# Narrower waits on the tensor engine, an interleaved first down product, and a second queue for x

## The reference

```python
h = rmsnorm(x, norm_mix_w);  proj = h @ w_in                # 24 groups of 512 columns here
go, S = gated_delta(conv(q,k,v), g, beta, S0)               # 8 heads, matrix state S
mh, C, n, m = mlstm(q, k, v, i, f, C0, n0, m0)              # 8 heads, state C and row n
mixed = sigmoid(gate_a) * (go @ w_branch_a) + sigmoid(gate_b) * (mh @ w_branch_b)
x = x + mixed @ w_out
f = rmsnorm(x, norm_ffn_w)
u, new_ffn_conv = causal_dwconv(f @ w_up, state_ffn_conv, ffn_conv_w)
x = x + (silu(u_gate) * u_val) @ w_down
y = rmsnorm(x, norm_final_w)                                # and all states are outputs
```

## Time and profile before

| | us |
|---|---|
| median of 3 runs | 1937.2 |
| the three runs | 1937.20, 1937.06, 1938.79 |
| the profiled execution's own time | 1938.22 |
| its span in the trace | 1936.3 |
| PE busy | 1898.7 (98%) |
| DVE busy | 1198.0 (62%) |
| ACT busy | 931.5 (48%) |
| mean granted clock of PE | 0.996 |

### The profile page before, as it was taken

How to read it: one execution, slowest core, us unless ns; L and a number is a source line. 1 busy time by engine, 2 the same in 40 slices (tenths; PEclk the granted TensorE clock), 3 DMA queues, 4 the chain that set the end, 5 groups by cost and what they waited for, 6 DMA issues and landing times.

```text
span 1936.3 us, 39112 instructions
## 1 busy us (share of the span) xinstructions
PE 1898.7 (98%) x14356; PEld 1855.5 (96%) x14356; DVE 1198.0 (62%) x2534; ACT 931.5 (48%) x1859; POOL 155.5 (8%) x324
## 2 busy tenths in 40 slices
PE   9999999999999999999999999999999999999996
PEld 8899999999999999999999999999999999999996
DVE  5766666666655666656655676754566664466742
ACT  5555455545534444445544544443454443354553
POOL 4000010001000110100022000000000000000021
PEclk9999999999999999999999999999999999999998
DMA  8555455555556666745755666656566656556552
GB/s 224 148 134 151 131 143 152 151 140 137 143 145 171 189 160 175 193 145 165 216 156 159 166 165 164 162 156 170 159 176 159 168 158 170 164 147 174 159 153 70
DMA packets 572607, 308.19 MB, mean 159 GB/s; under 512 B 10531, under 2 KB 567739, under 8 KB 572491
## 3 DMA queue, kind: packets, MB, share of 16 engines
q1 hardware_dynamic: 531943, 281.50, 53.6%
q10 hardware_dynamic: 40548, 25.13, 4.5%
HBM read 293.58 MB, written 13.02 MB: 158 GB/s over the span
## 4 chain that ended last, share of the span: by engine, by line
PE 83%; DVE 7%; issue 5%; ACT 4%; ACTq 1%; DVEq 1%; DMA 0%; SPq 0%; POOL 0%
PE products L1801 25%; PE products L1803 24%; PE products L1802 24%; PE mixer L1782 3%; DVE w_lo L585 2%; ACT w_hi L578 2%; PE mixer L1912 1%; PE mixer L1918 1%; DVE u_gate L1700 1%; DVE u_val L1700 1%; DVE u_padded L1690 1%; PE products L1986 0%; PE products L1960 0%; PE mixer L1864 0%; ACT conv_out L926 0%
## 5 line engine op out<-in xcount | busy, mean ns | idle before, releaser
L585 DVE TENSOR_TENSOR w_lo<-w_raw,w_hi 128x512 fp32r<-128x512 f32 x1037 | 717.6, 707 | 642.4 <-ACT w_hi L578 639.0
L578 ACT ACTIVATE w_hi<-w_raw 128x512 fp32r<-128x512 f32 x1037 | 628.5, 626 | 600.2 <-PE products L1803 572.5
L1801 PE MATMUL products<-h_hi,w_hi 128*128 128x288 f32 x1536 | 476.5, 310 | 0.0
L1802 PE MATMUL products<-h_lo,w_hi 128*128 128x288 f32 x1536 | 453.0, 295 | 0.0
L1803 PE MATMUL products<-h_hi,w_lo 128*128 128x288 f32 x1536 | 452.6, 295 | 0.0
L1801 PE MATMUL products<-f_hi,w_hi 128*128 128x288 f32 x1408 | 416.9, 296 | 0.0
L1802 PE MATMUL products<-f_lo,w_hi 128*128 128x288 f32 x1408 | 415.4, 295 | 0.0
L1803 PE MATMUL products<-f_hi,w_lo 128*128 128x288 f32 x1408 | 414.5, 294 | 0.0
L1801 PEld LDWEIGHTS products<-h_hi,w_hi 128*128 128x128 f32 x1536 | 289.2, 188 | 14.5 <-issue 10.4
L1802 PEld LDWEIGHTS products<-h_lo,w_hi 128*128 128x128 f32 x1536 | 289.1, 188 | 0.5
L1803 PEld LDWEIGHTS products<-h_hi,w_lo 128*128 128x128 f32 x1536 | 288.9, 188 | 0.0
(11 more groups left out here) (462 smaller groups left out, 2218.9 us busy)
## 6 DMA issues: line engine op xcount, KB each, us to landing
w_raw<-in_w_in SPq DMA_DIRECT2D x95, 1024.0 KB, 6.0
w_raw<-in_w_up SPq DMA_DIRECT2D x88, 1024.0 KB, 5.8
w_raw<-in_w_down SPq DMA_DIRECT2D x32, 1024.0 KB, 5.8
w_raw<-in_w_out SPq DMA_DIRECT2D x16, 1024.0 KB, 7.0
w_raw<-in_w_down SPq DMA_DIRECT2D x16, 768.0 KB, 4.8
w_raw<-in_w_branch_a SPq DMA_DIRECT2D x8, 1024.0 KB, 5.4
w_raw<-in_w_branch_b SPq DMA_DIRECT2D x8, 1024.0 KB, 5.5
S_sample<-in_state_gdn_S ACTq DMA_DIRECT2D x8, 512.0 KB, 7.4
```

What stands on the lines that cost most here:

```text
L578: nc.scalar.activation(ring_slot(whi, whi2, n, ring), raw[:, s % slots, 4 * j:4 * j + 4], ACT.Copy).then_inc(hi_ready, 1)
L585: nc.vector.tensor_tensor(ring_slot(wlo, wlo2, n, ring), raw[:, s % slots, 4 * j:4 * j + 4], ring_slot(whi, whi2, n, ring).bitcast(F32), A ...
L1801: mm(out, w_hi, x_hi, start=start, stop=False)
L1802: mm(out, w_hi, x_lo, start=False, stop=False)
```

## The change

Six edits, all in the order and in the waits of instructions; no arithmetic changes and only the order in which blocks are added into two banks differs.

1. **Start.** The eight small x loads of the samples are issued by ACT's queue, behind `norm_rows`; SP keeps the prompt's x and the weights.
2. **v_new.** ACT's copy of the first `v_new` becomes a lane of its own, ahead of `prepare`; the load of `S_sample` moves one slot later (`yield 1`).
3. **n.** PE turns n after the `ffn_w_rows` at the end of `w_out`, into banks 2 and 3; ACT copies and stores it there. PE's waits for the mLSTM's last steps move to the first uses (DVE's at the second product of a branch iteration, ACT's behind the branch stage), and `norm_sum` waits for `no_a.after("s")`.
4. **f_hi.** The five residual copies get a semaphore of their own (`ox_a`), and `turn_input` and the turn of `ffn_w_rows` wait for that one.
5. **down.** In the first group of each down product the first two column tiles are interleaved: (tile, j) runs (0,0) (0,1) (0,2) (1,0) (1,1) (1,2) (0,3) (1,3), then tiles 2 and 3 as before. ACT and DVE split the blocks in that order; DVE adds tile 0 up behind block 7 and tile 1 behind block 8; the reload of the first raw buffer waits for block 8 in place of 4 (6 in place of 3 in the last chunk).
6. **Loops.** For that, the last up iteration and the first down group of chunks 0 and 1 stand as straight-line code on ACT and DVE (the down group on PE, all four on SP), where they were loop passes.

```diff
@@ start @@
-                sp.dma_start(x_rows[0:TS, 2, cc], xs_rows[:, cc]).then_inc(x_in[g], 16)
-                sp.dma_start(xs4[:, g], xs_rows[:, cc].rearrange("t (m p) -> m t p", p=P)).then_inc(x_in[g], 16)
@@ ACT, behind the load of norm_rows @@
+            for g in range(4):
+                cc = slice(g * NG, (g + 1) * NG)
+                act.dma_start(x_rows[0:TS, 2, cc], xs_rows[:, cc]).then_inc(x_in[g], 16)
+                act.dma_start(xs4[:, g], xs_rows[:, cc].rearrange("t (m p) -> m t p", p=P)).then_inc(x_in[g], 16)
@@ ACT, lanes @@
+            def scan_begins(h):
+                yield 0
+                act.wait_ge(*scan_t.after("T0", h))
+                nc.scalar.activation(vn[0][:], bw[:, 0:P], ACT.Copy).then_inc(*scan_a.done("vn0"))
             def scan(h):
-                yield 0
+                yield 1
                 act.wait_ge(ss_out, 32 * h)
                 act.dma_start(ss[:], a["state_gdn_S"][0][:, h].rearrange("b k v -> k b v")).then_inc(ss_in, 16)
-                act.wait_ge(*scan_t.after("T0", h))
-                nc.scalar.activation(vn[0][:], bw[:, 0:P], ACT.Copy).then_inc(*scan_a.done("vn0"))
@@ PE, w_out @@
-                pe.wait_ge(*ot_a.before(i))
+                pe.wait_ge(*ox_a.before(i))
...
-            pe.wait_ge(*ot_a.before(4))
+            pe.wait_ge(*ox_a.before(4))
             for j in range(FC):
                 last = turn(pm[:, 1, j * 2 * FT:(j + 1) * 2 * FT], fw_rows[:, j], 2 * FT)
             last.then_inc(*n2_t.done("w"))
+            turn(pm[0:NB * H, 2, 0:P], n_s[:].rearrange("p b h -> p (b h)"), P)
+            turn(pm[0:H, 3, 0:P], n_p[:], P).then_inc(*no_t.done("tr"))
@@ order of blocks, ACT, DVE and PE @@
+        def late(n):
+            order = [(s, j) for s in range(2) for j in range(n - 1)] + [(s, n - 1) for s in range(2)]
+            return order + [(s, j) for s in range(2, 4) for j in range(n)]
@@ PE @@
+            def down_first(q, g, n, visits, x_last):
+                for b, (m, j) in enumerate(late(n)):
+                    if j == 0:
+                        pe.wait_ge(bank_free, 4 * g + (m + 1))
+                    if j == n - 1:
+                        pe.wait_ge(*x_last)
+                    pe.wait_ge(lo_ready, 16 * q + (b + 1))
+                    hi, lo = ring_slot(whi, whi2, b, 8), ring_slot(wlo, wlo2, b, 8)
+                    for k in range(4):
+                        kk = 4 * j + k
+                        last = product(ps[:, m, 0:T], hi[:, k], lo[:, k], u_hi[:, kk], u_lo[:, kk], kk == 0, kk == 4 * n - 1)
+                    last.then_inc(blocks, 1)
@@ SP, down of chunks 0 and 1 @@
+                            if i == 1 and s == 0:
+                                sp.wait_ge(lo_ready, 16 * q + 8)
```

More of the change, by code:

```diff
@@ L1091, in weights @@
                 split_hi(0, slot + 3, 4)
-            front(act, weights, [Lane(0, gates_rows())] + [Lane(PREP_AT[h], prepare(h)) for h in range(H)]
+            front(act, weights, [Lane(0, gates_rows())] + [Lane(SCAN_AT[h], scan_begins(h)) for h in range(H)]
+                  + [Lane(PREP_AT[h], prepare(h)) for h in range(H)]
                   + [Lane(SCAN_AT[h], scan(h)) for h in range(H)] + [Lane(MLSTM_AT[0] - 6, mlstm_first())]
@@ L1174, in up @@
                     group(split_hi, 2 * i + q, column_tiles(gate_tap, silu), ring=8)
-                    group(split_hi, 2 * i + (q + 1), column_tiles(value_tap, nothing, nothing, upper), ring=8, tail_next=tail_next)
-                repeat(act, n, up, n == TAIL)
+                    group(split_hi, 2 * i + (q + 1), column_tiles(value_tap, nothing, nothing, upper), ring=8, then=n if last else 0)
+                repeat(act, n, up, True)
                 q += 2 * n
@@ L1200, in _ @@
                 if n == 4:
-                    with act.Fori(0, 4) as i:
+                    group(split_hi, q, (), last_rows_ffn(4 * c, g0), 0, ring=8, first=True)
+                    with act.Fori(1, 4) as i:
                         group(split_hi, i + q, (), last_rows_ffn(i + 4 * c, i + g0), 0, ring=8)
@@ L1730, in up, with down @@
                     group(split_lo, 2 * i + q, column_tiles(gate, gate_taps), ring=8)
-                    group(split_lo, 2 * i + (q + 1), column_tiles(value, value_taps, gated, rest), ring=8, tail_next=tail_next)
-                repeat(dve, n, up, n == TAIL)
+                    group(split_lo, 2 * i + (q + 1), column_tiles(value, value_taps, gated, rest), ring=8, then=n if last else 0)
+                repeat(dve, n, up, True)
                 q += 2 * n
                 g0 += n
-                def down(q_, tile, at=0, n=4):
+                def down(q_, tile, at=0, n=4, first=False):
                     def evacuate(m, done):
@@ L1740, in evacuate @@
                         tt(t, t, ps[:, m, 0:T], ALU.add).then_inc(bank_free, 1)
-                    return column_tiles(evacuate, n=n)
+                    return late_tiles(evacuate, n) if first else column_tiles(evacuate, n=n)
                 if n == 4:
-                    with dve.Fori(0, 4) as i:
+                    group(split_lo, q, down(q, 0, first=True), ring=8, first=True)
+                    with dve.Fori(1, 4) as i:
                         group(split_lo, i + q, down(i + q, 4 * i), ring=8)
@@ L2215, in visits @@
                             yield 0
-                    for i in range(4):
-                        pe_group(q, g + i, u_hi, u_lo, visits(i), 4 * n, ring=8, b0=4 * n * i, n=n, x_last=x_last)
+                    down_first(q, g, n, visits(0), x_last)
+                    for i in range(1, 4):
+                        pe_group(q, g + i, u_hi, u_lo, visits(i), 4 * n, ring=8, b0=4 * n * i, n=n)
                     pe.wait_ge(*y_a.after("q"))
```

80 lines of the change are left out of this document (46 added, 34 removed).

## The result

The changed kernel takes 1923.2 us (median of 4 executions, 1922.99 to 1924.21) against 1937.8 us for the kernel before (4 executions too). The ratio is 0.9927, with a 95% interval of 0.9915 to 0.9938: 14.6 us faster. I had said 1919.0, in a range of 1916.5 to 1924.5.

What follows compares the result with a forecast made beforehand. PE was taken as the bound throughout. 4.5 + 1.6 - 0.3 + 6.8 + 5.1 + 1.5 + 0.3 = 19.5 us off the profiled 1938.2 gives 1918.7; 18.0 off the median 1937.2 gives 1919.2. Forecast 1919.0, range 1916.5 to 1924.5.

Steps and rivals of the forecast that it cites:

- What bounds the kernel: Whole kernel: PE's matmul stream plus 37.6 us of PE idle; only idle or low-clock time can be won.
- v_new, 4.5: Seven PE waits for ACT's v_new copy, 3.6 us, go; 4.5 us won, bounds 1.5 and 5.3.
- the next step, `S`: DVE's copy PE needs after v_new: nothing to spare, 0 to 0.3 us may be given back for each head.
- The state load: Load of `S_sample`, about 2.2 us later: costs nothing; landing late in all eight heads makes the kernel slower (2%).
- n and the branch stage: Branch start: a 1.06 us stall and two turns go, 1.6 us won; turns return behind `ffn_w_rows`, -0.3.
- f_hi, 6.8: In `w_out`: four PE waits of 5.8 us plus 0.25 each go, 6.8 us won; bounds 5.8 and 6.8.
- The rival that POOL's sum ends as late: End of `w_out`: transposes or `norm_sum` wait for something else; at most 6.8 lost, 1924 to 1926 us; 7%.
- u_lo and the clock: Down products: three waits go, 5.1 us; the clock's fall behind the 2.09 us wait goes too, 1.5 us.
- The burst of weights: Down products: 2 MB reloaded together costs nothing; rival of late weights, 1922 to 1932 us, 5%.
- Start, 0.3 with bounds of -0.3 and 0.3: Kernel start: the second queue removes PE's 0.27 us wait for the second quarter of x; 0.3 us won.
- my first rival: The v_new wait becomes one for `S` or the state load; v_new gives 0.5, time 1923 us; 18%.
- The clock falls anyway, here or elsewhere: Granted clock still falls, in the down product or elsewhere, once or twice: 1920.5 to 1922 us; 6%.

Runs made afterwards that it cites:

- the kernel with one queue: Changed kernel with x loaded as before, all by SP's queue: 1918.2 us, ratio 0.9899 against the kernel before.
- the weights by ACT's queue: Changed kernel with all of x on SP's queue and the first weight unit's four quarters on ACT's: 1923.1 us.
- the filled kernel: Changed kernel, two queues kept, with 3 more warm-up products ahead of x's first transposes and 6 ahead of the second quarter's: 1921.0 us.
- the squares' rows latest: Changed kernel with all of x on SP's queue and `xs4` behind the second weight unit and the small constant rows: 1925.8 us.

## Why the prediction was right, and where it was wrong

- **What bounds the kernel: right.** 12 us of idle time went, and the time with it. Nothing else became the bound. I had said idle time of about 22 us; it is 25.3.
- **v_new, 4.5: right, 5.0 measured**, nearer the upper bound of 5.3. What I feared for the next step, `S`, shows as one wait of PE's weight loads of 0.3 us, which no matmul waited for. The copy `S` ends at 190.14 in the changed kernel, PE's load for it is at 190.48 (compare). The state load, which I put at 8.2 us to spare against a landing of 8.1, lands in 5.3 to 7.0 us (median 5.8) from its later place (compare): the margin grew.
- **n and the branch stage, 1.6 - 0.3: right in the sum, 1.57 - 0.19 by the landmarks (the medians show nothing)**, with one part wrong. The two transposes' 0.3 us was not won; the stall cost 1.6 and not 1.31. The gates' wait is 1.40 and not the 1.07 that I said would stay, for this reason.
- **f_hi, 6.8: right, 6.7 measured.** The rival that POOL's sum ends as late did not come; it had 0.75 us to spare where I had worked out 1.
- **u_lo and the clock, 5.1 + 1.5 = 6.6: right, 6.85 measured.** Less the 5.1 of the waits, which is itself partly my estimate, the clock is 1.7; the clock stood at half for 3.4 us, which costs the same 1.7. The burst of weights made no wait. The Trainium skill (TensorE: Matmul & The Clock Gate, "What's actually happening") says that the throttled state is the default and activity releases it. The windows agree in so far as the clock falls behind a wait and comes back while PE is at work, in the down product and at the start; but the granted clock reads 1.00 from the first window on, before PE has done anything.
- **Start, 0.3 with bounds of -0.3 and 0.3: the step that failed. It measured -6.0** (6.3 lost by the first landmark, 0.3 of it back by the branch stage). I had looked at what the second queue saves, at a small delay of rows, and at the wait of 0.27 us that it could remove. I had not asked when `xs4` would land behind the sample rows in ACT's queue, though PE's counter waits for it: in the second quarter it landed at 12.98 us, where PE's own rows were in by 9.51, and PE stood for it in both quarters. My bounds came from the wait that was there: nothing in them asked what a later landing would cost, and what I had priced in the down product, that the clock falls behind a gap, I did not apply to the start. I had feared that the small rows delay the large ones; it was a small one that was late. The Trainium skill (DMA: Bandwidth & Descriptors, "Issuing engines are not separate DMA queues") says that DMAs of all engines run on the same 16 engines and interleave, whichever engine started them. The runs agree in so far as the second queue won nothing: 1918.2 and 1918.4 us with it, where it does not hold PE up, against 1918.2 without. I had let the rule change the sum by 0.3 us.
- **The range and the rivals.** The time missed my own forecast's 1917 to 1921. That it lies in the whole range is luck: the upper part of it was made for a smaller gain from the waits and for a failing v_new, and neither came. (That end was added up wrongly too: 1922.2 with v_new at 0.5 in place of 3.6 is 1925.3, not 1924.) The time came out at the 1923 of my first rival, but not by its mechanism: no wait took the place of v_new's. "The clock falls anyway, here or elsewhere" (1920.5 to 1922) came nearest, with half of the cause. My sum without the start, 19.5 - 0.3 = 19.2 us won, is met by the kernel with one queue: 19.7 us.

The change without its two queues takes 1918.2 us, 5.0 under the changed kernel, and no kernel tried is clear of it on the fast side. Three others lie within 0.2 us of it.

## What to carry to other kernels

Before loads are moved to another queue, list what each waiting counter counts, and ask of every load in it when it lands in its new place. Here PE's counter held a load that PE does not read, issued behind PE's rows in the second queue, and that load set PE's start. What is issued on the side can also delay the rows themselves, as with the weights by ACT's queue. Give every gap that an edit may open on TensorE the price of the clock too, which here about doubled it. And size edits of 1 to 5 us by the start of the same instruction in two traces, stage by stage: these add up here, where differences of medians did not.

## What the runs showed of the hardware that I had not expected

- The 14 warm-up products (28 passes) took from 5.09 to 6.23 us in different kernels though nothing in them differs and the granted clock reads 1.00 throughout. In the kernel before, the windows of 0.5 us show 4 to 5 passes each up to 6.0 us and 6 or 7 from there (a pass across a window's edge counts in both); in the changed kernel it stays at 4 to 5 until the last at 8.2. The following landmarks hardly move with it: the kernels with 5.1 and with 6.2 us reach `diag_of_sums` at 33.97 and 34.01 us.
- The length of PE's gap does not tell whether the clock falls, nor for how long. At the start it fell 2.1 us behind a wait of 0.90, 0.7 us behind one of 1.71 and 0.7 us behind one of 2.17, for 10.2, 10.2 and 6.8 us; behind one of 1.17 (the filled kernel) and one of 2.54 (at 31.73 us, with the squares' rows latest) it did not fall, and it was down for 3.4 us behind 2.09 (down product) and behind 3.85 (at 39.07 us). In the filled kernel PE had come to its faster rate at 6.0 us, in the changed kernel it had not by the first wait; whether this matters was not tried.
- The eight state loads land in 5.8 us (median) when they are issued one weight copy later, against 7.4 before.
- Of two 64 KB loads issued one behind the other on ACT's queue in the changed kernel, at 3.02 and 3.38 us, the first (PE's rows, 16 updates) was in by 9.51 us and the second (`xs4`, four updates) from 11.77 to 12.98. By one queue, issued at 3.60, `xs4` was in by 9.89. Whether its four parts, its place in the queue or the other queue's load makes the difference was not tried.
